# Roots of three norms multiplied in behind the products, and two norms in a row made one

## The reference

```
def rms_norm(x, g):
    y = x * rsqrt(mean(x * x, -1) + 1e-6)
    return y * g

# block 1, each of 2 layers l
h  = rms_norm(x, norm1_g[l]) * (1 + sc1) + sh1
x  = x + gt1 * merge_branches(attention(h @ w_in[l]), ...)
h2 = rms_norm(x, norm2_g[l]) * (1 + sc2) + sh2            # "n2"
x  = x + gt2 * ((silu(h2 @ w_gate) * (h2 @ w_up)) @ w_down)
# the context tokens take the same way in layer 0 only
x  = rms_norm(x, final_norm_g)                            # "nf"

# block 2, each of 2 layers l
z  = rms_norm(x, norm_w_2[l]) @ w_in_2[l]                 # "nw"
x  = x + three_branches(z) @ w_out_2[l]
x  = rms_norm(x, final_norm_w_2)                          # "fw"
```

## Time and profile before

| | us |
|---|---|
| time, median of 3 runs (2282.61 to 2288.09) | 2284.94 |
| time of the profiled execution | 2283.03 |
| its span | 2281.6 |
| TensorE busy | 2058.5 |
| VectorE busy | 952.3 |
| ScalarE busy | 876.6 |
| GpSimd busy | 664.2 |
| waits of TensorE for the last step of a root | 49.2, 26 times |
| waits of TensorE for the last sum of squares | 35.9, 8 times |

### The profile page before, as it was taken

The page is one execution under the profiler, slowest core; times in us unless marked ns, Lnnn a source line. Parts: engine busy times, 40 slices in busy tenths (PEclk is TensorE's granted clock), DMA queues, the critical chain, the costliest instruction groups (busy, mean ns, idle before and its releaser), DMA issues.

```text
span 2281.6 us, 30554 instructions
## 1 busy us (share of the span) xinstructions
PE 2058.5 (90%) x12588; PEld 1709.6 (75%) x12588; DVE 952.3 (42%) x1716; ACT 876.6 (38%) x1488; POOL 664.2 (29%) x297
## 2 busy tenths in 40 slices
PE   4899999998999999889988997988987889899786
PEld 1565667676788888677778997977877788778686
DVE  2424322364111111435455445467334645843555
ACT  1212333352321222334454443455452444644432
POOL 1221111233444444231123442423232333222322
PEclk7899999999999999989998998999998999999988
DMA  7423444521222322232224564533332444243231
GB/s 267 162 74 139 140 146 177 212 74 65 93 93 84 110 93 86 76 107 75 65 84 145 181 203 147 167 111 120 102 102 79 135 148 148 76 134 105 93 100 58
DMA packets 76554, 272.26 MB, mean 119 GB/s; under 512 B 8192, under 2 KB 11392, under 8 KB 76416
## 3 DMA queue, kind: packets, MB, share of 16 engines
q1 hardware_dynamic: 72576, 264.27, 34.5%
q10 hardware_dynamic: 3840, 6.04, 0.7%
HBM read 269.23 MB, written 1.05 MB: 118 GB/s over the span
## 4 chain that ended last, share of the span: by engine, by line
PE 74%; DVE 15%; ACT 5%; issue 2%; DMA 2%; POOL 2%; ACTq 0%; DVEq 0%; POOLq 0%
PE bank L745 20%; PE bank L746 18%; PE bank L747 18%; PE bank L904 4%; PE bank L928 3%; DVE low L1507 2%; PE bank L826 2%; PE bank L915 2%; DVE xc L1554 2%; ACT high L1141 2%; PE bank L867 1%; DMA xc<-ctx_in 1%; PE bank L893 1%; PE bank L838 1%; POOL few L1458 1%
## 5 line engine op out<-in xcount | busy, mean ns | idle before, releaser
L1449 POOL TENSOR_TENSOR low<-raw,high 128x1024 fp32r<-128x1024 f32 x260 | 627.3, 2415 | 1418.1 <-ACT high L1141 1418.1
L745 PE MATMUL bank<-h,high 128*128 128x256 f32 (+1 forms) x2432 | 807.5, 332 | 58.4 <-DVE h L1646 12.7
L746 PE MATMUL bank<-h,high 128*128 128x256 f32 (+1 forms) x2432 | 766.4, 315 | 0.0
L747 PE MATMUL bank<-h,low 128*128 128x256 f32 (+1 forms) x2432 | 765.5, 315 | 0.0
L745 PEld LDWEIGHTS bank<-h,high 128*128 128x128 f32 x2432 | 473.0, 195 | 158.4 <-issue 60.3
L746 PEld LDWEIGHTS bank<-h,high 128*128 128x128 f32 x2432 | 474.3, 195 | 29.6 <-issue 2.4
L747 PEld LDWEIGHTS bank<-h,low 128*128 128x128 f32 x2432 | 472.8, 194 | 29.7
L1141 ACT ACTIVATE high<-raw 128x1024 fp32r<-128x1024 f32 x408 | 426.8, 1051 | 145.8 <-PE bank L747 118.3
L1507 DVE TENSOR_TENSOR low<-raw,high 128x1024 fp32r<-128x1024 f32 x148 | 198.8, 1343 | 223.1 <-ACT high L1141 222.9
L1261 ACT ACTIVATE prob<-bank,small 128x512 f32<-128x512 f32 (+1 forms) x96 | 59.2, 617 | 187.4 <-DVE small L1690 111.2
L745 PE MATMUL bank<-hid,high 128*128 128x512 f32 (+1 forms) x352 | 118.2, 336 | 0.0
(11 more groups left out here) (262 smaller groups left out, 2671.9 us busy)
## 6 DMA issues: line engine op xcount, KB each, us to landing
raw<-stream SPq DMA_DIRECT2D x504, 512.0 KB, 3.4
xc<-x_in ACTq DMA_DIRECT2D x1, 1024.0 KB, 17.1
xc<-ctx_in ACTq DMA_DIRECT2D x1, 1024.0 KB, 28.5
out<-xc ACTq DMA_DIRECT2D x1, 1024.0 KB, 4.8
cst<-consts ACTq DMA_DIRECT2D x1, 960.0 KB, 29.0
cst<-consts ACTq DMA_DIRECT2D x1, 704.0 KB, 22.5
ukw<-uk ACTq DMA_DIRECT2D x1, 512.0 KB, 3.3
uvw<-uv ACTq DMA_DIRECT2D x1, 512.0 KB, 4.2
```

Of the source, the lines that this page charges most:

```text
L745: mm(dst, wh, xh, start=start, stop=False)
L746: mm(dst, wh, xl, start=False, stop=False)
L747: return mm(dst, wl, xh, start=False, stop=stop)
L1449: tt(low[:, i % PAIRS, :], raw[:, slot % SLOTS, :], high[:, i % PAIRS, :].bitcast(F32), ALU.subtract).then_inc(S["lo_pool"], 1)
```

## The change

The root of a norm is one number per token, so it can be multiplied in behind a product instead of in front of it: (x g root) @ W = root (x g @ W). This is done for three norms: `n2` of layer 1, `nw` 0 and `nw` 1. The moving operand of their products is gain x activation, made by a new step `gain` as each piece of `xc` is drained (ScalarE: high part, Identity with the gain as scale; VectorE: low part, one scalar_tensor_tensor of xc, gain and high part). For n2 the shift must not be scaled by the root, so it rides along as two extra columns (one for each modulation, 258 instead of 256) and comes out as a column of the bank.

`norm_late` replaces `norm_root` and `norm_tiles`: one tile of the next stage, then the last `sqsum` and `mean`, two more tiles, then `bcast`, a copy of the root to SBUF (`rsb`, ScalarE), and the drains kept back so far (`root_known`). All drains of X, DQ, SQ, SK, CV, Z, MO and MG, and of FG and FU in layer 1, are now on VectorE: bank x root. SV and MV, with tokens on partitions, take the root as ScalarE's scale. `nf` and `nw` 0 are one norm: `nf` sums the squares of x and of x times final gain in one pass (512 columns), and a step `again` gets the second root from the first and the second mean; `nf`'s own eight `norm` steps, which block 2's residual needs, stand behind the sixth X tile. `block2` stands in front of the last two X tiles. The weight splits are no longer held at these three norms. The output of `mix3` goes into buffers of its own (`merged`), over a part of the gates, instead of into h2. Unchanged: `n1` of both layers, `n2` of layer 0, `fw`, and all head norms.

```diff
 DRAIN = dict(K="act", Q="act", G="act", PA="dve", PB="dve", O="dve", FG="act", FU="dve", FD="dve",
-             X="act", DQ="act", SQ="act", SK="act", CV="act", Z="act", MO="act", MG="act", BR="dve", O2="dve",
+             X="dve", DQ="dve", SQ="dve", SK="dve", CV="dve", Z="dve", MO="dve", MG="dve", BR="dve", O2="dve",
              V="act", SV="act", MV="act")
+def scaled_late(stage, layer):
+    return stage in ("X", "DQ", "SQ", "SK", "CV", "Z", "MO", "MG") or stage in ("FG", "FU") and layer == 1
...
             if k == blocks - 1:
+                if scaled_late(stage, layer):
+                    if self.later is None:
+                        self.step("drain", stage, layer, j)
+                    else:
+                        self.later.append(("drain", stage, layer, j))
                 evac()
                 self.swept(self.sweeps)
...
+    def norm_late(m, sums, tiles):
+        o.later = []
+        o.run(next(tiles))
+        o.step("sqsum", sums, KT - 1)
+        o.step("mean", sums)
+        o.run(next(tiles))
+        if sums[0] == "nf":
+            o.step("again", sums)
+            o.run(next(tiles))
+        o.run(next(tiles))
+        o.step("bcast", sums)
+        o.step("rsb", m)
+        o.root_known()
...
     def second(l):
-        norm_root(("nw", l))
-        norm_tiles(("nw", l))
-        for j in range(6):
-            o.run(o.linear("X", l, j))
+        tiles = (o.linear("X", l, j) for j in range(6))
+        norm_late(("nw", l), ("nw", l) if l else ("nf", 0), tiles)
+        if not l:
+            o.step("block2")
+        for tile in tiles:
+            o.run(tile)
+        if not l:
+            for k in range(KT):
+                o.step("norm", ("nf", 0), k)
...
         for j in range(KT):
             def evac(j=j):
+                if l == 0:
+                    o.step("gain", after, j)
                 norm_sums(after, j)
-                o.hold = j == KT - 1
+                o.hold = l == 1 and j == KT - 1
             o.run(o.linear("O2", l, j, evac))
...
     for l in range(N_LAYERS):
         first(l)
-    norm_root(("nf", 0))
-    for k in range(KT):
-        o.step("norm", ("nf", 0), k)
-    o.step("block2")
-    for k in range(KT):
-        norm_sums(("nw", 0), k)
...
+                if stage in ("FG", "FU") and l:
+                    pe.wait_ge("gain", no["gain", ("n2", l), k])
+                    pe.wait_ge("shift", 1)
+                    return hh[:, k, 0:n + 2], hl[:, k, 0:n + 2]
...
+                elif kind == "gain":          # ScalarE
...
+                    do(hi, xc[:, k, 0:SEQ], ACTF.Identity, scale=g).then_inc(S["gain_hi"], 1)
+                elif kind == "rsb":
+                    m = key[0]
+                    act.wait_ge("bcast", no["bcast", root_of(*m)])
+                    do(rs_all, banks[7][:, 0:SEQ], ACTF.Copy).then_inc(S["rsb"], 1)
+                elif kind == "drain" and key[0] == "FG":
+                    stage, l, j = key
+                    act.wait_ge(*drained[key])
+                    do(gt[l][j % 2][:, :], gt[l][j % 2][:, :], ACTF.Silu,
+                       bias=shift_col[:, j % 2:j % 2 + 1]).then_inc(S["gate_out"], 1)
...
+                elif kind == "drain":         # VectorE
+                    stage, l, j = key
+                    ps = banks[bank_of["lin", stage, l, j]][:, 0:SEQ]
+                    dve.wait_ge("rsb", no["rsb", late_norm(stage, l)])
+                    dve.wait_ge("tile", work.sweep_of[key])
...
+                    elif stage == "Z":
+                        tt(Z[l][:, j, :], ps, rs_all, ALU.mult).then_inc(S["drained_dve"], 1)
...
+                    elif stage == "FG":
...
+                        nc.vector.tensor_copy(shift_col[:, at:at + 1], banks[bank_of["lin", stage, l, j]][:, SEQ:SEQ + 1])
+                        tt(t, ps, rs_all, ALU.mult).then_inc(S["drained_dve"], 1)
+                    elif stage == "FU":
...
+                        nc.vector.tensor_copy(shift_col[:, at:at + 1], banks[bank_of["lin", stage, l, j]][:, SEQ:SEQ + 1])
+                        tt(u, ps, rs_all, ALU.mult).then_inc(S["drained_dve"], 1)
+                        dve.wait_ge(*drained[key])
+                        dve.wait_ge("gate_out", j + 1)
+                        stt(out=t, in0=u, scalar=shift_col[:, at:at + 1], in1=t, op0=ALU.add, op1=ALU.mult).then_inc(S["gate_in"], 1)
+                        dve.wait_ge("gate_in", j + 1)
+                        dve.wait_ge("hid_hi", FT * l + j + 1)
+                        tt(hid[l][1][:, j % FC, :], t, hid[l][0][:, j % FC, :].bitcast(F32), ALU.subtract).then_inc(S["hid"], 1)
                     elif stage == "CV":
                         u = ubuf[j % 2]
...
+                        tt(u[:, :], ps, rs_all, ALU.mult).then_inc(S["drained_dve"], 1)
...
+                elif kind == "again":         # GpSimd: a second power between the two groups
...
+                    tt(ms, banks[bank_of["norm", m]][:, 2:4], first, ALU.mult).then_inc(S["dve_own"], 1)
+                    tt(ms, ms, first, ALU.mult).then_inc(S["dve_own"], 1)
+                    ts(ms, ms, EPS, None, ALU.add).then_inc(S["var2"], 1)
+                    dve.wait_ge("pow2", 1)
+                    stt(out=ms, in0=ms, scalar=-0.5, in1=r, op0=ALU.mult, op1=ALU.mult).then_inc(S["dve_own"], 1)
+                    tt(ms, ms, r, ALU.mult).then_inc(S["dve_own"], 1)
+                    stt(out=r, in0=ms, scalar=1.5, in1=r, op0=ALU.add, op1=ALU.mult).then_inc(S["dve_own"], 1)
+                    tt(f[:, 12:14], r, first, ALU.mult).then_inc(S["dve_own"], 1)
+                    tt(rs_col[:, 0, :], r, first, ALU.mult).then_inc(S["root"], 1)
+                elif kind == "gain":
...
+                    dve.wait_ge("gain_hi", no[step])
+                    stt(out=lo, in0=xc[:, k, 0:SEQ], scalar=g, in1=hi.bitcast(F32), op0=ALU.mult,
+                        op1=ALU.subtract).then_inc(S["gain"], 1)
```

More of the change, by code:

```diff
@@ L155, in linear, with root_known @@
             yield
+    def root_known(self):
+        for s in self.later:
+            self.step(*s)
+        self.later = None
     def token(self, stage, layer, tiles, width):
@@ L320, in evac @@
                     if half:
+                        if last:
+                            o.step("gain", ("nw", 0), j)
                         norm_sums(after, j)
[L322 removed]
+                        o.hold = not last and j == KT - 1
                 o.run(o.linear("FD", l, KT * half + j, evac))
     def second(l):
[L326 to L329 removed]
+        tiles = (o.linear("X", l, j) for j in range(6))
+        norm_late(("nw", l), ("nw", l) if l else ("nf", 0), tiles)
+        if not l:
+            o.step("block2")
+        for tile in tiles:
+            o.run(tile)
+        if not l:
+            for k in range(KT):
+                o.step("norm", ("nf", 0), k)
         for j in range(4):
```

226 lines of the change are left out of this document (153 added, 73 removed).

## The result

The changed kernel takes 2307.4 us (median of 4 runs, 2301.4 to 2313.8) against 2286.3 us before (median of 4 runs, 2282.6 to 2288.1). The ratio is 1.0097, 95% interval [1.0071, 1.0122]: about 22 us slower, between 16 and 28. Forecast were 2300 us and +16.1.

What follows compares the result with a forecast made beforehand. TensorE, busy 90% of 2281.6 us, was taken as the bound. Norms -21.2, layer 1's FFN +9.9 and block 2 +27.4 sum to +16.1 us, so a median of 2300 us; range 2264 to 2321.

Steps and rivals of the forecast that it cites:

- MV's wait of 13 us: Sign in block 2: TensorE's wait for MV before absorb grows from 3.3 and 4.0 us to 13 or more, released by VectorE's Z drain.
- Block 2: Its 132 drains moved from ScalarE to VectorE were to cost 27.4 us in sum.
- the stick-breaking stretch's delay: In block 2's stick-breaking and top-k stretch, twelve tiles drained on VectorE were to delay its end by 4.5 us.
- At the gates: At block 2's output gates, MG drains behind VectorE's 3.44 us product: 3.6 us for TensorE, 2.5 a layer after 1.1 forgiven.
- the mLSTM's heads: In block 2, some seven drains, half in the chain of waits, less ScalarE's time gone: cost 1 us a layer, 2 together.
- The double norm: The two norms in a row between the blocks: 22.6 us, of which 9.3 remain and 13.3 are won.
- (b): At the three norms, the mean waits for the last squares queued behind weight low parts: 3.0 us, 4.3 at the double norm.
- The second root's wait: At the double norm, the second root misses its three tiles by 0 to 3 us, taken as 1.2.
- the half clock: After the waits at the norms TensorE starts again at half clock: 1.0 us each.
- the last k step: After the last O2 tile, VectorE's low part ends late: 3.4 us of waiting, bounds 0 and 4.5; in FD 0.
- B: Rival at O, O2 and layer 1's FFN: GpSimd's hold never falls on the new operations; faster, 2271 us; chance 0.15.
- The hid loop: In layer 1's FFN, VectorE's loop per tile pair becomes 5.97 us against TensorE's 5.46: cost about 9 us, bounds 0 and 13.

## Why the prediction came out as it did

The direction, the size within 8 us and the main mechanism were right; several terms were not, and they offset each other, so that the sum came out so near is in part luck. Of the signs named, MV's wait of 13 us and a double norm of 9 us did not come (8.1 and about 14), and n2 kept 6.7 us where more than 7 were named; the others came.

**Block 2: right in sum (25.0 measured, 27.4 forecast), shown by the drains alone (23.7 in the trace), wrong in its parts.** The MV wait was to reach 13 us; it reached 8.1. I had added the stick-breaking stretch's delay to VectorE's arrival at "rows" but left TensorE where it was. TensorE was held in that stretch itself (first score to absorb: +6.3 and +7.0 us, 4.5 forecast) and so came later to MV too. The section behind it, up to the last absorb, grew by 6.4 and 5.8 us, as forecast (5.7). At the gates 3.3 were lost in either layer (3.6 worked out), but the mLSTM's heads and the branches took 3.9 and 3.5 less, not 1.1 less 1: this term is about 0 in place of 7. What shortened them no run shows, and in the three executions with the code of before they differ by 1.5 us among themselves.

**The double norm: mis-sized.** 8.6 us won in its stage, 13.3 forecast. The failed step is (b), "4.3 at the double norm": the mean waited 6.75, since two of GpSimd's low parts in a row held VectorE over a weight low part and the 512-wide sum. The run without those splits took it to 0.7. The second root's wait was 1.1 (1.2 forecast), the half clock cost 1.7 (1.0 forecast, a size that no row gave). Another 0.8 is the spacing of this stage's first 249 matmuls, 116.7 ns where it was 113.3; the last 0.8 of the 4.7 missed has no place.

**n2 and nw 1: right mechanism.** Waits at the last k step of 1.96 and 2.40 us (3.4 forecast, bounds 0 and 4.5), at the mean of 1.2 and 1.3 (3.0 forecast, and less than its lower bound of 1.7); the half clock cost 1.4 at n2 and 2.8 at nw 1 instead of 1.0. By the Trainium skill, page "SBUF — State Buffer", section "SBUF: two separate sides", the port is locked for a whole instruction. The traces agree: at the gates 0.03 us decided whether VectorE's product took 3.41 us and GpSimd's 2.35, or 1.23 and 3.48. B, the hold never falls, is out. For n2 the stage gives +3.4 - 8.9 (the spacing, next paragraph) - 1.4 (hid) = -6.9 us, 4.7 forecast. The run with n2 undone gives nearly the same: 1.5 lost in the stage, though FG and FU ran at 116.7 ns in place of 120.0 (3.5 us) and the wait for hid was gone (1.4), together 6.4.

**The FFN of layer 1: the sum near (+3.4 with n2, +5.2 forecast) by luck, both terms wrong.** The hid loop was worked out as 5.97 us against 5.46, and it is 5.89, so its length was right. But TensorE's pair was not 5.46 any more but 5.76, and a loop that is 0.13 longer costs 1.4 us, not 9. What I did not foresee is that slower pair: matmuls every 120.0 ns in FG and FU (1056 of them) and 116.7 in FD (528), where both were 113.3, is 8.9 us, of which the columns' 0.9 were in the sum. "0.9 ns per matmul for two columns" itself fits the slope from 258 to 288; two columns past 256 can be 3.4. The Trainium skill, page "TensorE: Matmul & The Clock Gate", section "Back-to-back issue gap", says that the spacing in a stream is set by weight load and matmul together; its formula for a single gap, N / 2.4 + 2.5 ns, would be an estimate of 109 ns at 256. The traces have 113.3 to 117.9 there, each steady over tens of us, and no run shows what chooses between them.

**What is not accounted for.** About 5 us of the 24 in the profiled execution lie ahead of the changed code and come and go between executions. The spacing's shift (5 to 8 us in this FFN, seen in all kernels with block 2's order or drains changed) is part of the 22 us in the medians. Every kernel here with a changed block 2 has it, also the one that only moves "rows", so it is no price of late roots; what it is a price of is not settled. The 0.4% by which the run with the gates' product moved was faster has no place in its trace either.

**The second forecast, that moving steps would win 4 to 8 us here and 8 to 13 there,** shows the same fault twice. Places where VectorE's queue holds TensorE are not a list of prices to be added: "rows" was worth 20.5 in its stages, the gates nothing in the trace, the held splits and "rows" together less than "rows" alone.

## What to carry to other kernels

Work that is moved from an engine with room to one that runs in program order costs little by its sum and much by what it queues behind: find, for each moved drain, the longest step ahead of it that itself waits for another engine, and move that step first. Here this one move made the kernel before 0.4% faster and took 8.7 us off what the drains cost in block 2. The other 16.3 us stayed, most of them in a stretch that grew by about as much as VectorE was given (6.3 us for 6.8); they use up the change's own gain at the three norms, which was real (6.9 + 8.6 + 2.4 = 17.9 us, 21.2 forecast). When a loop's length is compared with another engine's, take that engine's pace from a profile of the new kernel, or give it a range of some per cent.

## What was unexpected of the hardware

- The start-to-start time of the same 128x256 fp32r matmuls at granted clock 1.00 has steady levels that differ from program to program: 113.3 ns in three executions of the kernel before (one with a fill more), 116.6 to 117.9 in four others at 256 columns. It came back unchanged in a second execution of the same program. Moving one step that runs some 180 us after this stretch, and adding a fill there, was enough to change it.
- One more moving column costs 0.45 ns (258 to 288); going from 256 to 258 costs 3.4 ns at most.
- The same product of 128x1024 on VectorE took 1.23 us when it started 0.01 us ahead of GpSimd's (which then took 3.48) and 3.41 when it started 0.03 us behind one of 2.35. So an order that looks worse can be 2.2 us faster at one place.
